# Experts' token rows built on chip by 0/1 matrices instead of a scatter to HBM, a fetch per expert and a turn

## The reference

```python
expert = g_idx[:, None] * EXPERTS_PER_GROUP + top_i        # two of 32 experts for each token
dest = pad_start[sorted_e] + arange(a) - start[sorted_e]   # a slot for each (token, expert)
xs = x_pad[slot_token].reshape(n_blocks, MOE_BLOCK, D)     # rows gathered by expert
def expert_block(xb, e):
    hdn = silu(xb @ w_gate[e]) * (xb @ w_up[e])            # 1024 -> 512, twice
    return hdn @ w_down[e]                                 # 512 -> 1024
ys = map(expert_block, xs, block_expert)
y = segment_sum(ys[dest] * top_w, token)                   # weighted sum of the two
```

## Time and profile before

| | |
|---|---|
| time, median of 3 runs | 3340.39 us |
| the three runs | 3333.77, 3341.43, 3340.39 us |
| span of the profiled execution | 3333.3 us |
| PE busy | 2806.4 us (84%) |
| DVE, ACT, POOL busy | 1275.1, 877.4, 1089.3 us |
| HBM read and written | 750.36 MB and 63.14 MB |

### The profile page before, as it was taken

The page is one execution under the profiler, slowest core; times in us unless marked ns, Lnnn a source line. Parts: engine busy times, 40 slices in busy tenths (PEclk is TensorE's granted clock), DMA queues, the critical chain, the costliest instruction groups (busy, mean ns, idle before and its releaser), DMA issues.

```text
span 3333.3 us, 35642 instructions
## 1 busy us (share of the span) xinstructions
PE 2806.4 (84%) x13137; PEld 1834.4 (55%) x13137; DVE 1275.1 (38%) x2356; ACT 877.4 (26%) x1211; POOL 1089.3 (33%) x508
## 2 busy tenths in 40 slices
PE   6889879998998987889985988885797886988885
PEld 3767757777776775568762333332684772333331
DVE  4632144345225224753343322223427443322223
ACT  0433322235334212522221111112225331111111
POOL 0267746632874342224321000001363651000000
PEclk9989989999999998989987999998898997998998
DMA  5545488862554352622247999999241567999997
GB/s 159 171 150 176 158 296 291 288 223 70 166 173 152 139 164 98 216 89 91 101 152 277 390 401 399 399 398 357 76 139 49 179 234 289 391 396 397 396 398 288
DMA packets 218797, 781.17 MB, mean 234 GB/s; under 512 B 15092, under 2 KB 16290, under 8 KB 168752
## 3 DMA queue, kind: packets, MB, share of 16 engines
q1 hardware_dynamic: 189856, 669.61, 54.7%
q0 software_dynamic: 28816, 109.88, 9.9%
HBM read 750.36 MB, written 63.14 MB: 244 GB/s over the span
## 4 chain that ended last, share of the span: by engine, by line
PE 52%; DMA 22%; DVE 13%; SPq 6%; POOL 4%; ACT 2%; issue 2%; DVEq 0%; POOLq 0%; ACTq 0%
PE banks L737 11%; PE banks L738 10%; PE banks L742 10%; DMA weight_ring<-in_moe_w_down 4%; SPq L606 4%; PE banks L1131 4%; DMA arena<-in_moe_w_gate 3%; POOL weight_ring_r L1737 3%; DMA x_transposed<-in_moe_w_up 3%; DMA weight_ring<-in_moe_w_up 3%; DMA weights_high<-in_moe_w_gate 3%; PE banks L1154 2%; DMA tokens_out<-in_moe_w_down 2%; PE banks L820 2%; PE banks L870 2%
## 5 line engine op out<-in xcount | busy, mean ns | idle before, releaser
L1737 POOL TENSOR_TENSOR weight_ring_r<-weight_ring,weights_high_r 128x2048 fp32r<-128x2048 f32 x136 | 620.8, 4573 | 510.4 <-ACT weights_high_r L1387 419.8
L1387 ACT ACTIVATE weights_high_r<-weight_ring 128x2048 fp32r<-128x2048 f32 x136 | 257.5, 1901 | 736.4 <-PE banks L742 325.3
L737 PE MATMUL banks<-weights_high_r,x_transposed_r 128*128 128x512 f32 x1008 | 401.2, 398 | 33.9 <-ACT weights_high_r L1387 9.9
L1882 POOL DMA_DIRECT2D moe_y<-arena x64 | 33.9, 530 | 938.1 <-DVE arena L2570 922.1
L742 PE MATMUL banks<-weight_ring_r,x_transposed_r 128*128 128x512 f32 x1328 | 325.2, 391 | 2.1 <-POOL weight_ring_r L1737 2.1
L1737 POOL TENSOR_TENSOR weight_ring_r<-weight_ring,gates_r 128x2048 fp32r<-128x2048 f32 (+1 forms) x60 | 270.8, 4523 | 135.0 <-ACT gates_r L1387 73.8
L742 PEld LDWEIGHTS banks<-weight_ring_r,x_transposed_r 128*128 128x128 f32 x1328 | 249.5, 188 | 57.2 <-POOL weight_ring_r L1737 5.5
L737 PEld LDWEIGHTS banks<-weights_high_r,x_transposed_r 128*128 128x128 f32 x1008 | 192.6, 191 | 88.5 <-issue 26.4
L1593 ACT ACTIVATE arena<-banks 64x1024 f32<-64x1024 f32 x64 | 65.4, 1021 | 598.0 <-PE banks L1131 598.0
L738 PE MATMUL banks<-weights_high_r,arena_r 128*128 128x512 f32 x520 | 205.7, 396 | 0.0
L2552 DVE TENSOR_TENSOR arena<-banks,arena 64x1024 f32<-64x1024 f32 x64 | 77.9, 1217 | 312.9 <-ACT arena L1593 312.9
(11 more groups left out here) (383 smaller groups left out, 4886.3 us busy)
## 6 DMA issues: line engine op xcount, KB each, us to landing
weight_ring<-in_moe_w_down SPq DMA_DIRECT2D x62, 1024.0 KB, 30.6
weight_ring<-in_w_in SPq DMA_DIRECT2D x56, 1024.0 KB, 5.2
weight_ring<-in_w_ada SPq DMA_DIRECT2D x48, 1024.0 KB, 7.3
weight_ring<-in_ffn_w_in SPq DMA_DIRECT2D x44, 1024.0 KB, 5.1
weight_ring<-in_dil_w_qkv SPq DMA_DIRECT2D x36, 1024.0 KB, 5.2
tokens_out<-in_moe_w_gate SPq DMA_DIRECT2D x34, 1024.0 KB, 29.8
arena<-in_moe_w_up SPq DMA_DIRECT2D x34, 1024.0 KB, 29.2
weight_ring<-in_moe_w_up SPq DMA_DIRECT2D x34, 1024.0 KB, 28.9
```

What stands on the lines that cost most here:

```text
L737: nc.tensor.matmul(banks[t][:, 0:width], xh, wh[:, k, :], start=k0 + k == 0, stop=False)
L1387: nc.scalar.activation(high(s, kn, width), slot(c, kn, width), ACT.Copy).then_inc(high_ready, 1)
L1737: nc.gpsimd.tensor_tensor(slot(c, kn, width, ring_r), slot(c, kn, width), high(s, kn, width), ALU.subtract).then_inc(low_ready, 1)
```

## The change

Nothing is scattered to or fetched from HBM any more. The normalised rows stay in SBUF (`XTOK`). DVE marks, for four experts at a time (EG = 4, so 256 slots), which row belongs in which slot: a 128 x 256 matrix of 0 and 1 for each row tile, from comparing a row of slot numbers with each token's two slots (`mark`). PE multiplies the rows with that matrix (`dispatch`): with the rows as the stationary operand the product is the experts' rows, already turned. For each group of four experts that is eight k-blocks times `tiles` products of 128 x 256, spread over the four stages of the group before; ACT copies them out of banks 4, 6 and 7 (`expert_rows`). Group 0 is made before expert 0.

```diff
+            def mark(layer, g):
+                ...
+                for t in range(tiles):
+                    ...
+                    v(ts(slots_, iota, at[0], None, ALU.is_equal))
+                    v(stt(slots_, iota, at[1], slots_, ALU.is_equal, ALU.add), spread_ready)
-                def turn_x(e, i):
-                    par = e % 2
-                    pe.wait_ge(xs_in[par], counted(pe, 16 * (layer * NE // 2 + e // 2 + 1) + 16 * i))
-                    ...
+                def dispatch(g, j):
+                    n = g * EG + j
+                    if n >= 3:
+                        pe.wait_ge(xg_ready, b + n - 2)
+                    for kt in (2 * j, 2 * j + 1):
+                        for t in range(tiles):
+                            if kt == 0:
+                                pe.wait_ge(spread_ready, N_EG * sum(all_tiles[:layer]) + g * tiles + t + 1)
+                            last = nc.tensor.matmul(pair_bank(n)[:, kt % 2 * EG * CAP:(kt % 2 + 1) * EG * CAP],
+                                                    x_block(t, kt), marks_of(g, t), start=t == 0, stop=t == tiles - 1)
+                for j in range(EG):
+                    dispatch(0, j)
+                for e in range(NE):
+                    gate_up(e, 0)
+                    if e > 0:
+                        turn_hidden(e - 1)
+                    gate_up(e, 1)
+                    if e // EG + 1 < N_EG:
+                        dispatch(e // EG + 1, e % EG)
+                    if e > 0:
+                        down(e - 1)
```

- The results of odd experts stand on partitions 64 to 127 and those of even ones on 0 to 63 (`own(e)`), so ACT's copy and DVE's sum use one buffer for each parity.
- The loops of 14 turns are written out on all engines.
- Slots 10 and 11 wait for `logits_ready`, and slot 14 is gone:

```diff
                 elif slots[c] >= 10:
-                    sp.wait_ge(route_ready, layer_now[0] + 1)
-                    sp.wait_ge(scatter_out, 16 * 2 * sum(all_tiles[:layer_now[0] + 1]))
+                    sp.wait_ge(logits_ready, sum(all_tiles[:layer_now[0] + 1]))
```

More of the change, by code:

```diff
@@ L291, in build_program @@
         gated, halves_ready, summed, y_half = (sem("expert_" + n) for n in ("gated", "halves", "summed", "y_half"))
-        ov = [{n: sem(f"over{i}_{n}") for n in ("x_in", "w_in", "xT", "xT_copied", "gate_up", "halves", "summed", "sigmoid", "gated", "y_half", "hidden",
+        ov = [{n: sem(f"over{i}_{n}") for n in ("marked", "marked_one", "moved", "w_in", "xT", "xT_copied", "gate_up", "halves", "summed", "sigmoid", "gated", "y_half", "hidden",
                                                "hiddenT", "hiddenT_copied", "down", "y_copied", "y_out")}
@@ new lines, in experts @@
+                say(misc_ask)
+                for e in range(NE):
+                    if e > 0:
+                        hidden_turned(e - 1)
+                    sums(e)
+                    if e % EG == 1 and e // EG + 2 < N_EG:
+                        mark(layer, e // EG + 2)
+                    hidden(e)
+                    if e > 0:
+                        y_sum(e - 1)
+                    if e == 1 and layer + 1 < DEPTH:
+                        prepare(layer + 1)
+                hidden_turned(NE - 1)
@@ L2863, in _, with picked, pick @@
                   act_req)
+                def picked(k):
+                    a = 184 + 12 * k
+                    return [small[:, a + 4 * m:a + 4 * m + tiles] for m in range(3)]
+                def pick(k, m, values):
+                    v(tt(tmp, (first, second)[k], values, ALU.mult))
+                    v(red(picked(k)[m], tmp, X, ALU.add))
+                for k in range(2):
+                    pick(k, 1, e_idx)
                 bank = turned_bank()
@@ L2868, in _ @@
                 count = ar(RT + 128 * 12 + tiles * NE, NE)
+                for k in range(2):
+                    pick(k, 0, ranks)
+                    place, expert_, _ = picked(k)
+                    past, row_ = (small[:, 212 + 4 * m:212 + 4 * m + tiles] for m in range(2))
+                    v(ts(past, place, float(CAP), float(4 * NE * CAP), ALU.is_ge, ALU.mult))
+                    v(stt(row_, expert_, float(CAP), place, ALU.mult, ALU.add))
+                    v(tt(row_, row_, past, ALU.add))
+                    a = ROWS + k * MAX_TILES * N_EG
+                    v(tt(route[:, a:a + tiles * N_EG].rearrange("p (t g) -> p t g", t=tiles), spread(row_, tiles, N_EG),
+                         group_start.unsqueeze(1).broadcast_to([P, tiles, N_EG]), ALU.subtract))
+                mark(layer, 0)
                 table = ar(RT + 128 * 16, NE * (n_blocks - 1)).rearrange("p (e j) -> p e j", e=NE)
@@ L2885, in _ @@
                 q_table = ar(RT + 128 * 21, tiles * (n_blocks - 1)).rearrange("p (t j) -> p t j", t=tiles)
-                for k, hot in enumerate((first, second)):
-                    picked = small[:, 184 + 12 * k:196 + 12 * k]
-                    for m, values in enumerate((ranks, e_idx, start.unsqueeze(1).broadcast_to([P, tiles, NE]))):
-                        v(tt(tmp, hot, values, ALU.mult))
-                        v(red(picked[:, 4 * m:4 * m + tiles], tmp, X, ALU.add))
-                    place, expert_, begin = (picked[:, 4 * m:4 * m + tiles] for m in range(3))
+                for k in range(2):
+                    pick(k, 2, start.unsqueeze(1).broadcast_to([P, tiles, NE]))
+                    place, expert_, begin = picked(k)
                     q, past, row_ = (small[:, 208 + 4 * m:208 + 4 * m + tiles] for m in range(3))
```

434 lines of the change are left out of this document (189 added, 245 removed).

## The result

| kernel | runs | median us | lowest to highest us |
|---|---|---|---|
| before | 4 | 3337.18 | 3333.77 to 3341.43 |
| after | 4 | 3239.18 | 3237.48 to 3241.80 |

The ratio of the times is 0.9701, with a 95% interval of 0.9689 to 0.9714: about 98 to 100 us less, inside the predicted range of 3205 to 3272 and 7 us above the predicted 3232. The profiled execution of after took 3241.8 us, its span is 3240.1.

What follows compares the result with a forecast made beforehand. Weight loads (DMA) were taken to bound the experts, a chain of waits the time ahead of them. Layer 0 -51 and layer 1 -57 gave -108 us: 3232 us for the median, range 3205 to 3272.

Steps and rivals of the forecast that it cites:

- Price of the fetch: In the experts, each fetch costs the weight loads 0.65 MB, 1.55 us, though it moves only 0.26 MB.
- Pace: In the experts, without the fetch the loads take 15.53 us an expert in place of 17.08: -43.2 us a layer.
- Start: Ahead of each layer's experts, the first refill of a load slot comes earlier: -10.9 us in layer 0, -13.6 in layer 1.
- PE's stage: PE's work per expert with dispatch takes 15.1 us in layer 0, just under the loads' 15.53, and 13.3 in layer 1.
- Written out, it is read while the DMA engines are full: Experts' loops written out as straight code: reading the added code beside full DMA engines costs 0.
- 3 us for two limits so close: Layer 0's end: PE and loads finish nearly together, 2251.1 and 2252.9 us, so 3 us are added to the later.
- From there to the end of the layer the queue is never empty: Load queue: after the first refill, the layer's end is that moment plus the loads left times their pace.
- At nothing: Parts of the change put at 0, among them ACT's copies, DVE's marks in later stages, and stores from the upper half.
- the stepped copies: Eight copies in layer 0, four in layer 1, reading banks in steps: 0 to +8 us in all, taken as 0.
- the zeros: The zeros at 1339.6 us, moved while no weights do: 0 to -3 us, taken as 0.
- Rival (a): PE bounds layer 0, at 0.55 us a product: about -28 us there, -83 in all, 3257 us; chance 0.2.
- sum for PE alone: Layer 0 if PE never waited for loads: start, expert stages and last hidden row's way end at 2251.1 us.

Runs made afterwards that it cites:

- after_half_products: The kernel after with only row tiles 0 and 1 multiplied in layer 0's dispatch from group 1 on, 4 products a stage for 8; 3231.64 us, ratio 0.9666.
- rotate14: The kernel after with slots 12 and 13 kept in the load rotation, 14 in turn instead of 12 and two used once; 3230.34 us, ratio 0.9676.
- before_no_fetch: The kernel before with rows fetched only for experts 0 and 1 of each layer; scatter, turns, slots and loops stay; 3249.24 us, ratio 0.9718.
- after_fetch: The kernel after with one unread 64-row fetch per expert by POOL and the write of zeros to HBM put back; 3335.01 us, ratio 0.9982.

## Why the prediction was right, and where it was off

The mechanism and the largest terms held; the sum was 8 us too large. Layer by layer, with the 0.9 us of new instructions ahead of the copy of the ranks counted in: layer 0 -46.2 us where I had -51, layer 1 -53.6 where I had -57; together -99.8 against -108. (By the medians it is -98.0. The time itself came within 7 us of 3232, and not 10, because before's median fell from the 3340.39 that the prediction started from to 3337.18 with a fourth run.) The stretches before, between and behind the layers moved by no more than their scatter: from the last down product of layer 0 to the ranks of layer 1, for one, it is 457.5 us in before and 453.1 in after, and 451 to 458 in the other kernels.

- **Price of the fetch, 1.55 us: right** (1.42 to 1.65 in two kernels and two layers, over the 30 and 31 counted above). The prediction took it from three short windows, with no cause. The experiments narrow the cause to where the rows land. The Trainium skill (SBUF — State Buffer, Door 1: The DMA port swizzle) states that partitions 0 to 63 reach only 8 of the 16 SBUF ports that DMA uses; by its table of ports, every second partition reaches all 16. By that rule (0.262 MB at the 218 GB/s it gives for 8 ports, an estimate of 1.2 us) the spread-out fetch is cheap and the packed one dear. The runs agree in direction, 0.6 against 1.5 to 1.65 us, and the measured price is above the estimate. They agree for writes into SBUF alone: the section makes no difference between the directions, but a store out of 64 partitions cost 0.5 to 0.6 us, its bytes. No trace here shows a port. The rule of the Trainium skill that the prediction weighed (DMA: Bandwidth & Descriptors, Anatomy of one DMA), bytes over 436 GB/s or 0.6 us, holds here for the two other shapes and for stores.
- **Pace, 15.53 us an expert: right.** 15.51 without the fetch in the kernel before, 15.56 in after.
- **Start: right to 1.4 us.** Refill 12.3 us nearer in layer 0 (predicted 10.9), 12.7 in layer 1 (13.6). Marks at 0.35 + 0.48 a tile, with gaps 0.9 as predicted, 64 records of dispatch in 15.63 us, which is 32 x 0.43 and the 1.8 us that I added for the clock.
- **PE's stage: right.** 15.2 us (15.1); a dispatch 3.65 (3.5). PE waited for no load from 1850 to 2200 us and for nearly each late in layer 1, as the last part of the prediction said.
- **"Written out, it is read while the DMA engines are full ... so I put it at 0": this step failed.** It costs 3.0 and 2.8 us in the kernel before, and if it costs the same in after, most of the 8. The evidence I took for it, a stage of PE without a gap, could not show it. It was the stage of expert 3, which already ran in the loop; and PE would not have shown it, as it had loads in hand there and it is the weights that fall behind. The Trainium skill (Runtime: NRT & Kernel Launch, Instruction fetch mechanics) would have had it gain or be even; it came out slower, and the measurement decides.
- **3 us for two limits so close: too small.** Layer 0 lost about 3 more. after_half_products gets 3 to 4 us back by making PE faster, and rotate14 nearly 5 by bringing the last loads earlier.
- **"From there to the end of the layer the queue is never empty": not so.** Behind the first refill the DMA engines move 395, 287 and 370 GB/s in the three stretches of layer 0 shown above, and 379 in 20 us of layer 1, where 422 is full. In layer 1 closing the gap is worth 3.5 us. The old order of slots has such a gap as well (before_no_fetch moves 311 GB/s from 2777 to 2787 us), so little of it is in the difference that was predicted.
- **At nothing: the stepped copies held, and the zeros as far as can be seen.** Two copies of 128 x 512 take 1.42 us, stepped (L2789) as before (L2816). The zeros are back in after_fetch, and its ranks stand where the others' do; one profile can't tell 0 from the 3 us that the prediction allowed.
- **Slips that change nothing.** Rival (a) adds up to -28 - 57 = -85 and 3255 us, not -83 and 3257. By the prediction's own sum for PE alone, layer 0 stops winning at 0.67 us a product, not 0.69, as the start grows with it. All traffic came to 0.422 MB/us, not "near 0.415".
- **The later routing** that the first profile of after showed is scatter, as far as 14 profiles tell, and not an effect of the change.

## What to carry to other kernels

Where a stream of loads fills the DMA engines, price every other transfer by what the stream loses around it, and look at which partitions it touches: 64 rows side by side, written into SBUF, cost two and a half times the same rows on every second partition. Count written-out code as traffic there too. Where two kernels' profiles differ in code that is the same, compare from a common mark, and take more profiles before naming a cause.

## What was not expected of the hardware

- 256 KB into one half of the partitions cost the weight stream 1.5 to 1.65 us, into all or every second 0.6, and out of one half 0.5 to 0.6.
- The same fetch in the queue of the weights, into both halves in turn, cost 2.7 to 2.9 us, more than in POOL's, and no run says why.
- With 0.19 MB of code read beside it the weight stream lost about 0.5 MB in 350 us, to be taken with the 0.40 MB by which two like kernels differ.
- The start of layer 0's routing moves by 11 us among 14 profiles of kernels that are nearly alike ahead of it, and the runs of before reach from 3329.5 to 3349.0 us.
